# Two attentions of a two-block kernel: heads taken in twos, their weighted values alternating on the two column halves of the array

## What is computed

```python
logits = jnp.einsum('bqhd,bkhd->bhqk', qf[:, q0:q1], kf[:, :q1]) * scale
bias = c[:, :, q0:q1, None] - c[:, :, None, :q1]
logits = jnp.where(mask[None, None], logits + bias, NEG)
p = jax.nn.softmax(logits, axis=-1)
outs.append(jnp.einsum('bhqk,bkhd->bqhd', p, vf[:, :q1]))
```

```python
s = jnp.einsum('bqhd,bkhd->bhqk', qn, kn) + jnp.einsum('bqhd,bkd->bhqk', qr, kr)
p = jax.nn.softmax(s.astype(jnp.float32) * ATTN_SCALE, axis=-1).astype(v.dtype)
return jnp.einsum('bhqk,bkhd->bqhd', p, v)
```

## Time and profile before

| | us |
|---|---|
| median of three runs (3098.03 to 3105.61) | 3104.56 |
| the profiled execution | 3101.59 |
| its span in the trace | 3100.3 |
| PE busy | 2728.9 (88%) |
| DVE busy | 1579.3 (51%) |
| ACT busy | 658.5 (21%) |
| POOL busy | 560.6 (18%) |
| mean granted TensorE clock | 0.958 of 2.4 GHz |

### The profile page before, as it was taken

One profiled execution on the slowest core, in us unless ns is written; L12 is line 12 of the kernel. 1 busy time (PEld: TensorE's weight loads), 2 busy tenths in 40 slices (PEclk: granted clock), 3 DMA queues, 4 the chain that ended last, 5 costly groups with the idle time before them and its releaser, 6 DMA issues.

```text
span 3100.3 us, 23799 instructions
## 1 busy us (share of the span) xinstructions
PE 2728.9 (88%) x8266; PEld 1413.0 (46%) x8266; DVE 1579.3 (51%) x3526; ACT 658.5 (21%) x1599; POOL 560.6 (18%) x523
## 2 busy tenths in 40 slices
PE   8998999999998999899988888898898777777776
PEld 4674446666444444344456335543454323223222
DVE  1105325443106981255535583757647586757554
ACT  2114310001001002245421121122212221222112
POOL 0000000000000000000002333343334444434332
PEclk9997799999999999999999889999999999999999
DMA  3220013433211221000138999999999999999997
GB/s 133 96 82 1 21 55 136 163 136 136 102 75 62 82 76 48 14 1 1 55 136 336 386 352 394 381 396 400 392 392 376 390 420 420 420 420 420 420 420 317
DMA packets 88310, 702.06 MB, mean 226 GB/s; under 512 B 10088, under 2 KB 10728, under 8 KB 12928
## 3 DMA queue, kind: packets, MB, share of 16 engines
q0 software_dynamic: 73728, 536.90, 42.9%
q1 hardware_dynamic: 12416, 158.60, 13.2%
q10 hardware_dynamic: 2048, 5.03, 0.5%
HBM read 698.40 MB, written 2.10 MB: 226 GB/s over the span
## 4 chain that ended last, share of the span: by engine, by line
PE 60%; DMA 23%; DVE 11%; ACT 4%; issue 1%; POOL 1%; ACTq 0%; DVEq 0%; POOLq 0%
PE psum L346 35%; DMA slot<-in_experts,expert 12%; PE psum L878 11%; DMA weights<-in_experts,expert 11%; PE psum L726 2%; DVE slot L1809 2%; PE psum L671 2%; DVE weights L1809 1%; PE psum L811 1%; PE psum L795 1%; PE psum L513 1%; PE psum L780 1%; PE psum L734 1%; ACT spare_row L1268 1%; PE psum L480 1%
## 5 line engine op out<-in xcount | busy, mean ns | idle before, releaser
L878 PE MATMUL psum<-slot,spare_row 128*128 128x512 f32 x1096 | 529.6, 629 | 144.5 <-ACT spare_row L1268 144.5
L878 PE MATMUL psum<-weights,spare_row 128*128 128x512 f32 x952 | 453.7, 621 | 134.5 <-ACT spare_row L1268 134.4
L1809 DVE CUSTOM_DVE_ANT_0 slot<-slot,hT 128x1024 f32<-128x1024 f32 x274 | 333.1, 1223 | 231.3 <-DMA slot<-in_experts,expert 226.6
L346 PE MATMUL psum<-xnT,weights 128*128 128x257 f32 (+2 forms) x1568 | 424.0, 432 | 2.8 <-DVE xnT L1317 2.8
L878 PEld LDWEIGHTS psum<-slot,spare_row 128*128 128x128 f32 x1096 | 209.9, 199 | 431.7 <-issue 219.3
L1863 POOL DMA_INDIRECT weights<-in_experts,expert x238 | 255.7, 1075 | 763.6 <-DVE expert L1775 382.5
L1809 DVE CUSTOM_DVE_ANT_0 weights<-weights,hT 128x1024 f32<-128x1024 f32 x238 | 289.6, 1222 | 198.8 <-DMA weights<-in_experts,expert 198.1
L1863 POOL DMA_INDIRECT slot<-in_experts,expert x274 | 301.8, 1101 | 478.6 <-PE psum L878 464.1
L878 PEld LDWEIGHTS psum<-weights,spare_row 128*128 128x128 f32 x952 | 179.4, 197 | 389.7 <-issue 203.4
L346 PEld LDWEIGHTS psum<-xnT,weights 128*128 128x128 f32 x1568 | 298.9, 191 | 118.5 <-issue 82.2
L1263 ACT ACTIVATE coef<-hidden 128x2 f32<-128x2 f32 (+1 forms) x257 | 52.3, 203 | 1062.7 <-DVE hidden L1809 1062.6
(11 more groups left out here) (324 smaller groups left out, 2618.5 us busy)
## 6 DMA issues: line engine op xcount, KB each, us to landing
weights<-in_w_mod SPq DMA_DIRECT2D x12, 2048.0 KB, 8.5
weights<-in_w_pq SPq DMA_DIRECT2D x12, 2048.0 KB, 11.7
weights<-in_w_up SPq DMA_DIRECT2D x11, 2048.0 KB, 7.6
weights<-in_w_out SPq DMA_DIRECT2D x8, 2048.0 KB, 9.7
weights<-in_w_in SPq DMA_DIRECT2D x8, 2048.0 KB, 8.3
weights<-in_w_o_mla SPq DMA_DIRECT2D x6, 2048.0 KB, 10.7
weights<-in_w_in_t SPq DMA_DIRECT2D x4, 2048.0 KB, 8.0
weights<-in_w_down SPq DMA_DIRECT2D x4, 2048.0 KB, 7.7
```

The source lines that it names most:

```text
L346: last = pe.matmul(out, lhsT, rhs, start=start and n == 0, stop=stop and n == len(pairs) - 1)
L878: last = pe.matmul(acc.pair[:, half, :], k.diags[pick % 8], k.slots[slot][:, D + half * 512:D + (half + 1) * 512], start=h0 == 0 and j == ...
L1809: ins = dve.tensor_tensor_reduce(slot[:, 0:D], slot[:, 0:D], k.h2[:, i, :], 1.0, 0.0, ALU.mult, ALU.add, hid[:, j:j + 1])
```

## The change

Heads are taken in pairs. In both attentions the lists of items run tile by tile with the two heads of a pair alternating: (0, tile), (1, tile), (0, next tile) and so on.

In the first block a step now handles two items on every engine: PE issues the scores of both heads one after the other (for the 528-wide ones half by half, head by head), then both masks; then the transposes of the two items before; the values of a pair come two double steps behind its last scores, with the products of the two heads alternating for each key tile, and fill both halves of one PSUM bank. DVE's order in a double step becomes: maxima of both, copies of the two transposed items before, scalings of both. ACT copies a pair's values once, over 128 partitions. Biases are made two at a time.

In the second block the steps stay single. `probsT[q]` now holds, for queries 256q to 256q + 255, both heads of a pair; `values(p, q)` comes every four steps, for pair p and half q of the queries, with 256 streamed columns and the two heads alternating for each key tile. DVE's copy is 128x256 in place of 64x512. Since queries and keys are still made at tile 1 of an odd head, they move from step 16g + 13 to 16g + 11 and from 8p + 5 to 8p + 3.

```diff
...
+
+            both = []
+            for a in (c, c + 1):
+                width = META if items[a][1] == NT else items[a][3] + P
+                both.append(take(("fox_s", a), n=2 if width > BANK else 1))
             h, i, n, at = items[c]
-            rows = slice((h % 2) * FDH, (h % 2) * FDH + FDH)
-            q, key = k.fqk[rows, h // 2, :], k.fqk[rows, 4 + h // 2, :]
-            width = META if i == NT else at + P
-            u = take(("fox_s", c), n=2 if width > BANK else 1)
-            if i == NT:
-                pe.matmul(u.pair[0:n, 0, 0:n], q[:, 0:n], key[:, 0:n], start=True, stop=False)
-                last = pe.matmul(u.pair[0:n, 0, 0:n], k.ident16[0:n, 0:n], k.causal16[0:n, 0:n], start=False, stop=True)
-            elif width <= BANK:
-                pe.matmul(u.pair[:, 0, 0:width], q[:, at:at + n], key[:, 0:width], start=True, stop=True)
-                last = pe.matmul(u.pair[:, 0, at:width], k.ident16[:], k.causal16[:], start=False, stop=True, skip_group_check=True)
-            else:
-                pe.matmul(u.pair[:, 0, 0:HALF], q[:, at:at + n], key[:, 0:HALF], start=True, stop=True)
-                pe.matmul(u.pair[:, 1, 0:HALF], q[:, at:at + n], key[:, HALF:NK], start=True, stop=True)
-                last = pe.matmul(u.pair[:, 1, at - HALF:HALF], k.ident16[:], k.causal16[:], start=False, stop=True, skip_group_check=True)
-            last.then_inc(u.fill())
+            first, second = both
+            rows = [slice(0, FDH), slice(FDH, P)]
+            for half in range(2 if width > BANK else 1):
+                for u, r in zip(both, rows):
+                    q, key = k.fqk[r, h // 2, :], k.fqk[r, 4 + h // 2, :]
+                    if width > BANK:
+                        pe.matmul(u.pair[:, half, 0:HALF], q[:, at:at + n], key[:, half * HALF:(half + 1) * HALF], start=True, stop=True)
+                    else:
+                        pe.matmul(u.pair[0:n, 0, 0:width], q[:, at:at + n], key[:, 0:width], start=True, stop=i != NT)
+            for u in both:
+                if i == NT:
+                    last = pe.matmul(u.pair[0:n, 0, 0:n], k.ident16[0:n, 0:n], k.causal16[0:n, 0:n], start=False, stop=True)
+                elif width <= BANK:
+                    last = pe.matmul(u.pair[:, 0, at:width], k.ident16[:], k.causal16[:], start=False, stop=True, skip_group_check=True)
+                else:
+                    last = pe.matmul(u.pair[:, 1, at - HALF:HALF], k.ident16[:], k.causal16[:], start=False, stop=True, skip_group_check=True)
+                last.then_inc(u.fill())
...
-        def values(h):
-            rows = slice((h % 2) * FDH, (h % 2) * FDH + FDH)
-            pt = k.scoresT[h % 2]
-            u = take(("fox_v", h), n=2)
-            for c in range(5 * h, 5 * h + 5):
+        def values(p):
+
+            u = take(("fox_v", p), n=2)
+            for c in range(10 * p, 10 * p + 10):
                 pe.wait_ge(*ps.of["fox_t", c].free)
             for j, n, at in tiles()[1:] + tiles()[:1]:
-                v = k.fv[0:n, j, h * FDH:(h + 1) * FDH]
-                if j == NT:
-                    pe.matmul(u.pair[rows, 1, 0:META], v, pt[0:n, j, 0:META], start=True, stop=True)
-                    last = pe.matmul(u.pair[rows, 0, 0:SEQ], v, pt[0:n, j, META:NK], start=False, stop=True)
-                else:
-                    pe.matmul(u.pair[rows, 0, at - META:SEQ], v, pt[:, j, at:NK], start=j == 0, stop=False)
+                for h in (2 * p, 2 * p + 1):
+                    rows = slice((h % 2) * FDH, (h % 2) * FDH + FDH)
+                    v, pt = k.fv[0:n, j, h * FDH:(h + 1) * FDH], k.scoresT[h % 2]
+                    if j == NT:
+                        pe.matmul(u.pair[rows, 1, 0:META], v, pt[0:n, j, 0:META], start=True, stop=True)
+                    else:
+                        pe.matmul(u.pair[rows, 0, at - META:SEQ], v, pt[:, j, at:NK], start=j == 0, stop=False)
+            for h in (2 * p, 2 * p + 1):
+                rows = slice((h % 2) * FDH, (h % 2) * FDH + FDH)
+                last = pe.matmul(u.pair[rows, 0, 0:SEQ], k.fv[0:META, NT, h * FDH:(h + 1) * FDH], k.scoresT[h % 2][0:META, NT, META:NK], start=False, stop=True)
             last.then_inc(u.fill())
...
         bias(0)
-        for c in range(len(items) + 3):
+        bias(1)
+        for c in range(0, len(items) + 6, 2):
             if c < len(items):
...
                 h, i = items[c][0:2]
-                if i == NT - 1 and h + 1 < FH:
-                    bias(h + 1)
+                if i == NT - 1 and h + 2 < FH:
+                    bias(h + 2)
+                    bias(h + 3)
             if 0 <= c - 2 < len(items):
                 transposes(c - 2)
-            if c >= 3 and items[c - 3][1] == NT - 1:
-                values(items[c - 3][0])
+                transposes(c - 1)
+            if c >= 4 and c - 4 < len(items) and items[c - 4][1] == NT - 1:
+                values(items[c - 4][0] // 2)
...
         pe.wait_ge(s.ret_mixed, RH)
-        for h in range(FH):
+        for h in range(FH // 2):
             pe.wait_ge(*ps.of["fox_v", h].free)
...
         def scores(c):
-            h, i = divmod(c, NT)
+            h, i = k.heads_order[c]
             Q, K = k.Q[h // 4 % 2], k.K[h // 2 % 2]
...
-        def values(h):
-            rows = slice((h % 2) * VD, (h % 2) * VD + VD)
-            pt = k.probsT[h % 2]
-            u = take(("a_v", h))
-            if h == 0:
+        def values(p, q):
+
+            u = take(("a_v", p, q))
+            if p == 0 and q == 0:
                 for j in range(KT):
                     pe.wait_ge(*ps.of["values2", j].free)
-            for c in range(NT * h, NT * h + NT):
+            for c in range(8 * p + 4 * q, 8 * p + 4 * q + 4):
                 pe.wait_ge(*ps.of["a_t", c].free)
-            chain(u.pair[rows, 0, :], [(k.values[j][:, h * VD:(h + 1) * VD], pt[:, j, :]) for j in range(KT)]).then_inc(u.fill())
+            for j in range(KT):
+                for a in range(2):
+                    rows = slice(a * VD, (a + 1) * VD)
+                    last = pe.matmul(u.pair[rows, 0, 0:2 * P], k.values[j][:, (2 * p + a) * VD:(2 * p + a + 1) * VD], k.probsT[q][:, j, a * 2 * P:(a + 1) * 2 * P],
+                                     start=j == 0, stop=j == KT - 1)
+            last.then_inc(u.fill())
             return u
...
             if c < AH * NT:
-                h, i = divmod(c, NT)
+                h, i = k.heads_order[c]
                 scores(c)
...
                 transposes(c - 3)
-            if c >= 4 and (c - 4) % NT == NT - 1:
-                u = values((c - 4) // NT)
+            if c >= 4 and c % 4 == 3:
+                u = values((c - 4) // 8, (c - 4) // 4 % 2)
         k.ring_done[k.lent] = u.full[-1]
...
                     if g == 0 and n == 0:
-                        pe.wait_ge(*ps.of["a_v", 2 * c].free)
-                        pe.wait_ge(*ps.of["a_v", 2 * c + 1].free)
+                        pe.wait_ge(*ps.of["a_v", c, 0].free)
+                        pe.wait_ge(*ps.of["a_v", c, 1].free)
                     last = pe.matmul(u.pair[:, 0, 0:len(tiles_) * P], w[:, c, v * P:(v + 1) * P], k.heads[:, cut, c, :], start=c == 0, stop=c == KC - 1)
...
             if h > 1:
-                act.wait_ge(s.fox_nm, 5 * (h - 1))
+                act.wait_ge(s.fox_nm, 10 * (h // 2))
             copy_out(("fox_b", h), halves(k.raw[h % 2][:]), of["fox_b", h].pair[:, :, 0:HALF], scale=-1.0)
...
             if h > 1:
-                act.wait_ge(*of["fox_v", h - 2].full[-1])
+                act.wait_ge(*of["fox_v", h // 2 - 1].full[-1])
             if i == NT:
...
-        def values(h):
-            rows = slice((h % 2) * FDH, (h % 2) * FDH + FDH)
-            u = of["fox_v", h]
+        def values(p):
+            u = of["fox_v", p]
             act.wait_ge(*u.full[-1])
-            act.activation(k.mixedT[rows, 4 + h // 2, META:NK], u.pair[rows, 0, 0:SEQ], ACT.Copy)
-            act.activation(k.mixedT[rows, 4 + h // 2, 0:META], u.pair[rows, 1, 0:META], ACT.Copy).then_inc(u.out)
+            act.activation(k.mixedT[:, 4 + p, META:NK], u.pair[:, 0, 0:SEQ], ACT.Copy)
+            act.activation(k.mixedT[:, 4 + p, 0:META], u.pair[:, 1, 0:META], ACT.Copy).then_inc(u.out)
...
         bias(0)
-        for c in range(len(items) + 3):
+        bias(1)
+        for c in range(0, len(items) + 6, 2):
             if c < len(items):
                 exps(c)
+                exps(c + 1)
                 h, i = items[c][0:2]
-                if i == NT - 1 and h + 1 < FH:
-                    bias(h + 1)
+                if i == NT - 1 and h + 2 < FH:
+                    bias(h + 2)
+                    bias(h + 3)
             if 0 <= c - 2 < len(items):
                 transposes(c - 2)
-            if c >= 3 and items[c - 3][1] == NT - 1:
-                values(items[c - 3][0])
+                transposes(c - 1)
+            if c >= 4 and c - 4 < len(items) and items[c - 4][1] == NT - 1:
```

(43 more changed lines are left out.)

## The result

The changed kernel takes 3013.47 us (median, 3002.02 to 3017.8), the kernel before beside it 3104.73: ratio 0.9705, 95% interval 0.9678 to 0.9731. The profiled execution of the changed kernel took 3017.8 us, so between the two profiles lie 83.8 us; I account for those.

What follows compares the result with a forecast made beforehand. The prediction took PE to bound both attention stages. Savings of 30 + 8 + 20 = 58 us took the profiled 3101.6 us to 3043.6, and 3 us more for the median gave 3046, range 3018 to 3092.

Steps and rivals of the forecast that it cites:

- Everything overlapped: Both attentions: best case with every overlap in full, saving 86 us and giving 3019 us.
- Second attention, values: Second attention: two heads' values run at once on the column halves, a block taking 3.4 us, saving 30 us.
- what is left open is the weight load at the change of head: Second attention, values: each 64-column load stays exposed when heads alternate, 0.053 us per load.
- rows only: Rival, both attentions: row halves overlap, column halves don't; 12 us saved, 3093 us, chance 0.10.
- nothing overlaps: Rival, both attentions: no halves run at once and nothing is paid; 3 us saved, 3102 us, chance 0.08.
- the drain at each change of half: Rival, values of both attentions: each change of half drains the array, 0.1 us; 3131 us, chance 0.07.
- the upper bound: Second attention, values: the two halves overlap fully, a block falling from 5.33 to 2.67 us, 42.6 us saved.
- Order of queries: Second attention: queries at tile 11 rather than 13 avoid a wait and a low-clock block; 8 us saved.
- First block: First block's forgetting attention: values 16, scores 14 and order 3 us saved, 13 lost, 20 us net.
- the longer way round: First block: PE waits for DVE and ACT as pairs lengthen the chain, 3.3 us a pair, 13 us lost.
- The net of order and chain: First block: grouping two items saves 3 us of shape changes, the longer chain loses 13 us.
- The rival of the clock: Rival, first block: new gaps keep PE at 1.2 GHz, gaining nothing or losing 5 us; 3072 us, chance 0.10.

Runs made afterwards that it cites:

- serial_first: Changed kernel, but in the first block scores go head by head with the mask between, and one head's value products before the other's: 3031.64 us.
- serial_second: Changed kernel, but in each values block of the second attention all twelve instructions of one head stand before the other's: 3036.86 us.

## Why the prediction was wrong

The mechanism, two halves of the array at work at once, was right in both blocks, and all three terms were too small. "Everything overlapped" had been worked out at 86 us; the two attentions gave 83.1.

**Second attention, values: 30 forecast, 40.3 measured.** The step that failed is "what is left open is the weight load at the change of head", 0.053 us in each of 12 places of a block. The loads run under the matmuls, at a change of head as elsewhere, and two instructions start within 40 ns, so a block is 12 x 0.217 + 0.13 = 2.74. The 12 x 0.053 = 0.64 us a block are the whole miss of 10.3. The argument was at hand in the prediction itself, used against the rival: the load is hidden in before's blocks of 12. The rivals "rows only" and "nothing overlaps" and the drain at each change of half are refuted by the same block. The Trainium skill, "TensorE: Matmul & The Clock Gate", section "Measured speedup vs the span model", has a span model for narrower tiles which, carried over to two halves, gives the 42.6 us of the upper bound; the blocks agree with that within 0.07 us a block.

**Order of queries: 8 forecast, bound 10, measured 13.4.** I had counted 1.5 us of a wait and 1.7 of the low clock in each of three places. Both were right. Missed were the 0.5 us that a block usually waits, which the keys' products now cover, the same at the keys that come without queries, and 0.3 us ahead of the slow block, whose transposes started late (1366.79, where the rhythm had 1366.54). A step that is moved also fills the gap that it is moved into.

**First block: 20 forecast, 29.1 measured.** The 27.3 us of work saved are 39 us at before's clock of 0.70. Divided as in the table by kind, that is about 16 for scores (14 forecast), 18 for values (16 forecast, and the same step failed here: no load appears, the work is half), and 5 for the order (3 forecast). Against these 39 stand 5.3 of idle time and the lower clock (0.66 for 0.70), which took 52.5/0.66 - 52.5/0.70 = 4.5: 29.2. This is bookkeeping at one clock. In the time of the stage itself the serial kernel has 12.8 of the 29.1 us (some 5 of them the last products side by side, 4 a clock of 0.73), and alternating scores and values the other 16.3, where 30 were forecast for both.

The term of this block that was furthest off is the longer way round, "13 us lost", where idle time rose by 5.3. The stretches were there at about the places named: apart from the stage's start and its last wait, the waits of the changed kernel come to 9.7 us, 2.4 a pair where 3.3 were forecast. But before had 2.7 us of such waits too, which I hadn't taken off, and its wait at the start was 0.9 longer. Why the stretches are shorter than reckoned isn't shown. That PE ran at the low clock half of the time doesn't explain it: idle time is 15.5 us at a clock of 0.66, 18.0 at 0.70 and 17.9 at 0.75. The net of order and chain was put at a loss of 10, and `serial_first` gained 12.8 in the stage. The rival of the clock came true in small: it had 26 us at stake, and took 4.5.

What saves the 2 to 4 us in biases, masks and transposes isn't settled; fewer changes of shape is what I had, and no run tells them from the pairing of biases.

**From profile to median.** With these terms 58 becomes 58 + 10.3 + 5.4 + 9.1 = 82.8 us saved; the second attention has 0.3 more, the stage between 0.2 and the rest 4.3, and the start takes 3.8: 83.8. The median lies 4.3 us below the profiled execution, where I had added 3. That last step, 7 us of scatter between executions, is what put the result outside the range and not at its edge.

## What to carry to other kernels

Two products that use 64 of the array's columns, or 64 of its rows, run at once if their instructions stand close together; count a pair as one, weight loads included. How close was tested for the column halves alone: with three matmuls of one half waiting ahead of it the other half's still started, with more it waited. Where the granted clock of a stage is between its levels, reckon in work (busy time by clock) first, and only then in time: the work of several edits adds up, and the clock decides how much of it arrives. Look at what fills the gap behind a step that is moved, not only at what waited for it.

## What the runs showed of the hardware

- PE does not start matmuls in the order of the program when halves of the columns are used: in `serial_second` one passed three that waited, a block of 24 took 4.50 us where one after the other would be 5.3. The Trainium skill, "TensorE: Matmul & The Clock Gate", section "The mechanism", says that matmuls start and end in program order; the starts in this trace show otherwise (the ends are modelled, and show nothing).
- The same section has it that a weight load overlaps a running matmul where the row group differs, or into a background buffer. Here both heads' weights lie on all 128 rows, and the loads are hidden also at every change of half: 24 loads of 137 ns in a block of 2.74 us.
- Two 64-row halves are as independent as two 64-column halves: alternating the scores and alternating the values each saved 10 to 11 us of work in the first block, and both kinds ended at half of before (24.5 to 12.2 and 27.1 to 13.5 us).
- The same first block, instruction for instruction, ran at mean clocks of 0.66 to 0.75 in six profiles.
